# Second layer's rise of a fused mixer network: 18 of 22 pairs by seven block products for eight

## The chip, the cores and the metric

One core of one Trainium2 chip. The metric is the device time of one execution in microseconds, lower is better; a kernel's time is the median of its runs. TensorE is the matmul engine (PE in the profile), VectorE is DVE, ScalarE is ACT, GpSimd is POOL, and SyncE (SP) issues the weight transfers.

## What is computed

A first block (four mixers on 512 tokens of width 1024) and a second block of two layers; layer 0 of it also carries 256 context tokens, layer 1 works on the 512 tokens alone. Each layer of the second block ends with this part, and the change is in layer 1's:

```
h = rms_norm(x) * (1 + m4) + m3                 # 512 x 1024
z = h @ w_up                                    # 1024 x 5632, the "rise"
z = conv over tokens, width 3, per channel, + b
g, v = split(z)                                 # 2816 channels each
x = x + m5 * ((silu(g) * v) @ w_down)           # the "fall"
```

Everything is float32. Channels are taken in tiles of 128: a "pair" is a gate tile and its value tile, 22 pairs make the 2816 hidden channels.

## The kernel before

Channels lie on the partitions, tokens on the free axis. TensorE multiplies in a rounded form of float32, so every product is made of three (`three_products`, lines 225 to 227): each operand is split into a high part (a cast) and a low part (the rest), and high x high, high x low and low x high are added in PSUM. Weights come in *units* of 128 x 1024 (512 KB): all input channels for one tile of output channels, as eight weight tiles of 128 x 128. `stream_weights` (line 278) issues the units on SyncE's queue into a ring of four slots, each when a slot has been used. ScalarE casts a unit from the ring (`split_high`, line 479) into one of two buffers, VectorE subtracts (`split_low`, line 487) and thereby frees the slot.

`feed_forward` (lines 2684 on) is used for both layers. The rise has 44 units, gate and value tile of a pair in turn. A unit of layer 1 is 24 matmuls of 512 columns into one PSUM bank. VectorE then makes the convolution from the bank (centre tap with bias, line 2796, and two side taps, line 2801), ScalarE the Silu of a gate tile (line 2766), VectorE the product into `hidden` (line 2813). The first two units are opened in parts (lines 590 and 593), since h's high parts are ready before its low parts. VectorE makes h_low in line 430; before that stands the norm (line 425). The fall follows with 22 units, two of hidden's tiles at a time, in two halves of four banks; its moving operands are split two units ahead, and the results are added to x (line 2983) and stored. The order of work on each engine is the order in which the code emits it, all engines are in order, and every hand-over is a semaphore counted.

Elsewhere the change touches: the start of `build`, where POOL, once x and the constants are in, issues three tables (line 3138); behind that `recur_and_project`, where POOL issues `lora` (line 1399) and, after the normed x is split, `lru_w` (line 1401), for both of which TensorE waits at line 1455, after the third unit of steady work, ahead of the matmuls of lines 1459 and 1460; POOL's mask products in the scan stage (line 1629), two groups of chunks; and POOL's part of layer 0's feed-forward (silu_rows, lines 2718 to 2730, fetched again in line 2867).

## Time and profile before

| what | value |
|---|---|
| median of three runs | 2077.84 us |
| lowest, highest | 2071.98, 2082.45 us |
| the profiled execution, span | 2070.4 us |
| TensorE, VectorE, ScalarE, GpSimd busy | 97%, 63%, 36%, 4% of the span |
| granted TensorE clock, mean | 0.989 |
| weight loads (SyncE's queue) | 317 of 512 KB |

The page gives no time of the profiled execution beside its span, from its first to its last instruction; it is 1.6 us under the lowest timed run. Matmuls are pipelined: a matmul of 512 columns is drawn 0.39 us long and the next starts 0.23 us after it, so starts are what is to be compared. The granted clock is a share of the full 2.4 GHz. A row of a view that groups by line shows count, busy time, mean ns of one, and then the engine's idle time ahead of the group with what ended it.

### The profile page before, as it was taken

What the parts mean: (1) busy time and instruction counts of PE and PEld (TensorE: products, weight loads), DVE (VectorE), ACT (ScalarE), POOL (GpSimd) and SP (SyncE); (2) the same over time, 40 slices, a digit from 0 to 9 for tenths busy, and PEclk for the clock granted to TensorE, in tenths of its full rate; (3) what the DMA queues carried; (4) which work ended last, traced back from release to release, by engine and by line L of the source; (5) the groups of instructions that cost most, each with busy time, mean ns of one, the idle gap of its engine ahead of it and who ended that gap; (6) DMA issues with size and microseconds to landing.
All of it is one profiled execution on the core that took longest, in us unless ns stands there. A gap on an engine that the chain in (4) does not pass through costs nothing.

```text
span 2070.4 us, 29947 instructions
## 1 busy us (share of the span) xinstructions
PE 2014.7 (97%) x11473; PEld 1635.4 (79%) x11473; DVE 1296.3 (63%) x2091; ACT 738.3 (36%) x1188; POOL 84.1 (4%) x156
## 2 busy tenths in 40 slices
PE   7999999999999899999999999999999999999999
PEld 6677776577788678788888888887787778888887
DVE  6764424656548684688877664556477757766644
ACT  6621113744356452411111122334365432222332
POOL 0001000000130000000000000000310000000000
PEclk9989998999999999999999999999999999999999
DMA  5112125522362301233334233333543022223232
GB/s 200 64 62 103 62 103 183 197 88 84 134 176 65 127 1 51 92 109 129 128 128 134 83 112 122 102 112 102 156 129 118 4 89 83 100 91 101 94 100 81
DMA packets 57669, 217.43 MB, mean 105 GB/s; under 512 B 7440, under 2 KB 7440, under 8 KB 56416
## 3 DMA queue, kind: packets, MB, share of 16 engines
q1 hardware_dynamic: 46752, 168.32, 24.5%
q0 software_dynamic: 9296, 44.86, 6.7%
q10 hardware_dynamic: 1520, 2.85, 0.4%
q8 instruction: 72, 1.18, 0.2%
q14 instruction: 29, 0.24, 0.0%
HBM read 200.78 MB, written 15.20 MB: 104 GB/s over the span
## 4 chain that ended last, share of the span: by engine, by line
PE 88%; DVE 7%; ACT 3%; issue 2%; ACTq 0%; DVEq 0%
PE psum L225 23%; PE psum L226 22%; PE psum L227 22%; PE psum L816 3%; PE psum L590 2%; PE psum L777 2%; PE psum L804 2%; PE psum L1517 1%; PE psum L2013 1%; PE psum L2141 1%; PE psum L233 1%; PE psum L593 1%; PE psum L2547 1%; DVE neg_max L848 1%; PE psum L1543 1%
## 5 line engine op out<-in xcount | busy, mean ns | idle before, releaser
L225 PE MATMUL psum<-h_high,unit_high 128*128 128x512 f32 (+1 forms) x1704 | 620.6, 364 | 5.1 <-DVE unit_low L1390 4.5
L226 PE MATMUL psum<-h_low,unit_high 128*128 128x512 f32 (+1 forms) x1704 | 611.1, 359 | 0.0
L227 PE MATMUL psum<-h_high,unit_low 128*128 128x512 f32 (+1 forms) x1704 | 609.7, 358 | 0.0
L479 ACT CAST unit_high<-ring 128x1024 fp32r<-128x1024 f32 x196 | 205.4, 1048 | 563.6 <-PE psum L227 557.2
L225 PEld LDWEIGHTS psum<-h_high,unit_high 128*128 128x128 f32 x1704 | 322.1, 189 | 62.3 <-issue 5.3
L487 DVE TENSOR_TENSOR unit_low<-ring,unit_high 128x1024 fp32r<-128x1024 f32 x196 | 239.4, 1221 | 195.3 <-ACT unit_high L479 195.3
L226 PEld LDWEIGHTS psum<-h_low,unit_high 128*128 128x128 f32 x1704 | 322.4, 189 | 48.6 <-issue 2.8
L227 PEld LDWEIGHTS psum<-h_high,unit_low 128*128 128x128 f32 x1704 | 322.3, 189 | 48.6
L2801 DVE SCALAR_TENSOR_TENSOR conv_out<-psum,parameters,conv_out 128x511 f32<-128x511 f32 (+1 forms) x264 | 166.3, 658 | 21.3 <-DVE conv_out L2796 5.7
L2796 DVE TENSOR_SCALAR conv_out<-psum,parameters 128x512 f32<-128x512 f32 (+1 forms) x132 | 91.2, 719 | 113.4 <-PE psum L227 110.9
L889 ACT ACTIVATE probs<-psum,neg_max 128x768 f32<-128x768 f32 (+4 forms) x136 | 98.6, 728 | 129.4 <-DVE neg_max L848 117.2
L848 DVE TENSOR_REDUCE neg_max<-psum 128x1 f32<-128x768 f32 (+4 forms) x136 | 97.3, 740 | 27.6 <-PE psum L777 26.5
L816 PE MATMUL psum<-v,turned 128*128 128x64 f32 x784 | 99.2, 270 | 0.5 <-DVE v L866 0.5
L816 PEld LDWEIGHTS psum<-v,turned 128*128 128x128 f32 x784 | 96.0, 193 | 3.7 <-issue 1.8
L227 PE MATMUL psum<-y_high,unit_low 128*128 128x512 f32 (+1 forms) x256 | 93.6, 366 | 0.0
L225 PE MATMUL psum<-y_high,unit_high 128*128 128x512 f32 (+1 forms) x256 | 93.6, 366 | 0.0
L226 PE MATMUL psum<-hidden_part_low,unit_high 128*128 128x512 f32 (+1 forms) x264 | 93.5, 354 | 0.0
L226 PE MATMUL psum<-y_low,unit_high 128*128 128x512 f32 (+1 forms) x256 | 93.4, 365 | 0.0
L227 PE MATMUL psum<-hidden_part_high,unit_low 128*128 128x512 f32 (+1 forms) x264 | 93.1, 353 | 0.0
L225 PE MATMUL psum<-hidden_part_high,unit_high 128*128 128x512 f32 (+1 forms) x264 | 92.9, 352 | 0.0
L225 PE MATMUL psum<-unit_high,h_high 128*128 128x512 f32 x176 | 77.0, 438 | 0.0
L2766 ACT ACTIVATE conv_out<-conv_out 128x768 f32<-128x768 f32 (+1 forms) x44 | 32.6, 741 | 104.3 <-DVE conv_out L2801 104.3
(445 smaller groups left out, 2816.7 us busy)
## 6 DMA issues: line engine op xcount, KB each, us to landing
ring<-in_w_units SPq DMA_DIRECT2D x317, 512.0 KB, 3.5
stacked_heads<-head_parts POOLq DMA_DIRECT2D x48, 192.0 KB, 5.0
x_apart<-xT POOLq DMA_DIRECT2D x1, 3072.0 KB, 10.2
bias<-in_na_bias POOLq DMA_DIRECT2D x2, 1536.0 KB, 9.0
xT<-x_apart POOLq DMA_DIRECT2D x1, 3072.0 KB, 10.3
head_parts<-head_parts_high POOLq DMA_DIRECT2D x6, 384.0 KB, 6.2
head_parts<-p POOLq DMA_DIRECT2D x6, 384.0 KB, 6.0
xT<-in_x ACTq DMA_DIRECT2D x4, 512.0 KB, 6.0
```

Source lines behind the costliest of these rows:

```text
L225: pe.matmul(out, lh, rh, start=first, stop=False, skip_group_check=True)
L226: pe.matmul(out, lh, rl, start=False, stop=False, skip_group_check=True)
L227: return pe.matmul(out, ll, rh, start=False, stop=last, skip_group_check=True)
L479: act.copy(K.w_high[:, (K.unit + j) % 2], source).then_inc(K.high_split.sem, 1)
L487: dve.tensor_tensor(K.w_low[:, q % 2], K.ring[:, e % RING], K.w_high[:, q % 2].bitcast(F32), ALU.subtract).then_inc(K.unit_used.sem, 1)
L590: mm = pe.matmul(K.ps[bank][:, 0:b - a], high, moving[part][:, k, a:b], start=(k == 0 and part == 0), stop=(k == KD - 1 and part == 1), sk ...
L777: mm = pe.matmul(score_tile(t, c, c0, c0 + w), lhs, rhs, start=(g == 0), stop=(g == len(group) - 1), skip_group_check=len(group) > 1)
L816: mm = pe.matmul(K.ps[6][:, 0:HD], turned[:, t % 2, b * P:b * P + P], items[t]["v"](tile), start=(b == 0), stop=(b == len(tiles) - 1))
L848: max_ready.up(dve.reduce_max(neg_max[:, t, c:c + 1], score_tile(t, c, 0, kw), AX, negate=True))
L889: exped.up(act.activation(probs[:, t % depth, c, 0:kw], score_tile(t, c, 0, kw), ACT.Exp, bias=neg_max[:, t, c:c + 1], accum_out=row_sum[: ...
L2796: ins = dve.tensor_scalar(t(j, c0, c0 + w), bank[:, 0:w], column(wc + 44), column(bc), ALU.mult, ALU.add)
L2801: ins = dve.scalar_tensor_tensor(part, bank[:, src:src + w - 1], column(wc + 88 * (tap - 1)), part, ALU.mult, ALU.add)
```

## The change

18 of layer 1's 22 pairs leave the units. Their weights are cut in 2 x 2 blocks (input half by kind, gate or value), h in 2 x 2 blocks (input half by token half, 256 tokens), and a block product is made by Strassen's method in the form of Winograd: seven products instead of eight, with four sums of weight blocks (s1 = a21 + a22, s3 = a21 + a11, s2 = s1 + a11, s4 = s2 + a12; the signs are carried by h's sums and by the results) and four sums of h's blocks (T1 to T4). A *turn* takes two pairs, 7 *steps*; a step is 24 matmuls of 256 columns, 12 for each pair. The first four pairs stay whole units.

The weight sums are made in HBM by transfers of POOL's queue: copies of a21 to s1 and s3 right behind the three tables at the start, accumulations of a22 and a11 ahead of the second group of mask products, and in layer 0's feed-forward, behind silu_rows, copy and accumulation for s2 and then for s4, each waiting for the one before. T1 to T4 and their low parts are made by VectorE, their high parts by ScalarE, between norm and rise. Weight units of the rise have four buffers instead of two. Centre taps move from VectorE to ScalarE; results of the seven products go over three pairs of banks and are joined in a buffer `block_out`, from which the taps read. The fall is a function of its own, the same for both layers but for what its opening waits for. The rise of layer 1 is written out in full, with no hardware loop.

```diff
+SINGLE = 4
+TURN_PAIRS = 2
+B_TURNS = (KF - SINGLE) // TURN_PAIRS
+B_STEPS = 7
+LEFT, HALF_K = ("a11", "a12", "s2", "s1", "s3", "s4", "a22"), KD // 2 * P
+STORED, SUMMED = ("a11", "a12", "a21", "a22"), ("s1", "s2", "s3", "s4")
...
+            if n_units <= u < n_units + B_UNITS:
+                turn, step = divmod(u - n_units, B_STEPS)
+                if u == n_units:
+                    sp.wait_ge(K.signals["sums_made"].sem, 16 * len(SUMMED))
+                source = block_rows(K, LEFT[step])[TURN_PAIRS * turn:TURN_PAIRS * turn + TURN_PAIRS]
+                source, slot = source.rearrange("e p c -> p e c"), slot.rearrange("p (e c) -> p e c", e=TURN_PAIRS)
...
+def sum_blocks(K, pool, to, name, add):
+
+    rows = lambda x: block_rows(K, x).rearrange("t (q f) c -> (t q) (f c)", f=4)
+    if add:
+        return pool.dma_start(rows(to), rows(name), accum_op=ALU.add, max_dma_last_dim=8192)
+    return pool.dma_start(rows(to), rows(name))
...
     def _(pool):
         for g in range(NT // 2):
+            if g:
+                pool.wait_ge(sig["sums_copied"].sem, sig["sums_copied"].n)
+                for to, added_block in (("s1", "a22"), ("s3", "a11")):
+                    sig["sums_made"].up(sum_blocks(K, pool, to, added_block, True), 16)
             for lev in range(1, STEPS):
...
                 rows_out.up(pool.dma_start(K.silu_rows, rows_up[:, 0:2]), 16)
+                copied, made = K.signals["sums_copied"], K.signals["sums_made"]
+                for to, copy, addend in (("s2", "s1", "a11"), ("s4", "s2", "a12")):
+                    pool.wait_ge(made.sem, made.n)
+                    copied.up(sum_blocks(K, pool, to, copy, False), 16)
+                    pool.wait_ge(copied.sem, copied.n)
+                    made.up(sum_blocks(K, pool, to, addend, True), 16)
...
                 K.loaded_rest.up(pool.dma_start(dst, src), 16)
+            for to in ("s1", "s3"):
+                K.signals["sums_copied"].up(sum_blocks(K, pool, to, "a21", False), 16)
```

The new rise, engine by engine (`feed_forward_in_blocks`). TensorE, a turn:

```diff
+                    pe.wait_ge(K.unit_used.sem, first + n + 1)
...
+                    elif step == 1 and turn:
+                        pe.wait_ge(c11_out.sem, c11_out.base + turn)
...
+                    elif step == 2:
+                        pe.wait_ge(first_out.sem, first_out.base + turn + 1)
+                    elif step == 3 and turn:
+                        pe.wait_ge(c12_out.sem, c12_out.base + turn)
...
+                    elif step == 4:
+                        pe.wait_ge(second_out.sem, second_out.base + turn + 1)
+                    elif step == 5:
+                        pe.wait_ge(fifth_out.sem, fifth_out.base + turn + 1)
+                    elif step == 6:
+                        pe.wait_ge(c22_out.sem, c22_out.base + turn + 1)
...
+                    bank = (Y(turn), X, Y(turn), Z, Y(turn), Z, Y(turn))[step]
...
+                            mm = three_products(pe, K.ps[bank + e][:, 0:HS], (upper[:, c], lower[:, c]), x,
+                                                step in (0, 1, 3) and k == 0, k == KD // 2 - 1)
+                    product.up(mm)
```

VectorE's opening (T1 to T4 and the whole units), and its turn:

```diff
+            low(dve, 2)
+            side_tap.up(dve.tensor_tensor(total(T1), block(0, 0), block(0, 1), ALU.subtract))
+            link(dve, side_tap, dve.tensor_tensor(step_up, shift(4, 4), shift(0, 4), ALU.subtract))
+            for k in range(4):
+                side_tap.up(dve.scalar_tensor_tensor(total(T3)[:, k, :], block(1, 1)[:, k, :], step_up[:, k:k + 1],
+                                                     block(0, 1)[:, k, :], ALU.add, ALU.subtract))
+            low(dve, 3)
...
+            total_low(T3, 1.0, 2)
+            for n in range(2 * SINGLE):
+                taps(n // 2, n % 2, K.ps[n][:, :])
                 if n >= 2:
+                    low(dve, n + 2)
+                if n % 2:
+                    put_hidden(n // 2)
...
+                    if step == 5:
+                        unit_finished(dve, n - 1)
+                        dve.wait_ge(fifth_out.sem, fifth_out.base + turn + 1)
...
+                        c22_out.up(dve.scalar_tensor_tensor(C_out[:, 1, :, HS:S], both(Y(turn)), -1.0, fifth_part,
+                                                            ALU.mult, ALU.subtract))
+                    if step == 6:
+                        unit_finished(dve, n - 1)
+                        dve.wait_ge(second_out.sem, second_out.base + turn + 1)
+                        c12_out.up(dve.tensor_tensor(C_out[:, 0, :, HS:S], second_part, both(Z), ALU.add))
+                    if n + 2 < LAST:
+                        low(dve, n + 2)
...
+                    if step < 2 and turn:
+                        gate_tile(before, step)
+                    if step == 2 and turn:
+                        value_tile(before, 0)
+                    if step == 3:
+                        unit_finished(dve, n - 2)
+                        dve.wait_ge(first_out.sem, first_out.base + turn + 1)
...
+                        c11_out.up(dve.tensor_tensor(C_out[:, 0, :, 0:HS], first_part, both(X), ALU.add))
+                        if turn:
+                            value_tile(before, 1, (0,))
+                    if step == 4 and turn:
+                        value_tile(before, 1, (1,))
+                        put_hidden(SINGLE + TURN_PAIRS * before)
+                    if step == 5 and turn:
+                        put_hidden(SINGLE + TURN_PAIRS * before + 1)
```

ScalarE's opening and turn:

```diff
+            high(act, 2, None)
+            high(act, 3, None)
+            total_up(T1, 1.0, 1)
+            total_up(T3, 1.0, 6)
+            for n in range(2 * SINGLE):
+                unit_finished(act, n)
...
+                centre(n // 2, n % 2, K.ps[n][:, :])
+                if n < 2 * SINGLE - 1:
+                    high(act, n + 4, None)
+                if n % 2:
+                    soft(n // 2)
+                if n == 0:
+                    total_up(T2, -1.0, 10)
+                    total_up(T4, -1.0, 14)
...
+                    if step == 0 and turn:
+                        value_out(turn - 1)
+                    if step == 1:
+                        unit_finished(act, n - 1)
+                        act.wait_ge(c11_out.sem, c11_out.base + turn)
+                        first_out.up(act.copy(first_part, both(Y(turn))))
...
+                    if n + 3 < LAST:
+                        high(act, n + 3, n - 1)
...
+                    if step < 2 and turn:
+                        value_in(turn - 1, step)
+                    if step == 2 and turn:
+                        for e in range(TURN_PAIRS):
+                            soft(SINGLE + TURN_PAIRS * (turn - 1) + e)
+                    if step == 6:
+                        gate_in(turn)
```

## Rows read from the trace of the kernel before

**Rows 1.** The page, busy time and share of the span by engine
```profile
PE 2014.7 (97%) x11473; PEld 1635.4 (79%) x11473; DVE 1296.3 (63%) x2091; ACT 738.3 (36%) x1188; POOL 84.1 (4%) x156
```

**Rows 2.** The chain that ended last, from 1700 us on, shares by line
```profile
by line: PE psum L226 31.9%; PE psum L225 31.8%; PE psum L227 31.2%; PE psum L590 1.9%; PE psum L593 1.0%; DVE unit_low L487 0.3%; ACT unit_high L479 0.3%; DVE hidden L425 0.2%; DVE xT L2983 0.2%; ACT h_high L413 0.2%; ACT hidden L410 0.2%;
```

**Rows 3.** Windows: length; busy PE, PEld, DVE, ACT, POOL; PEclk, DMA share, GB/s
```profile
14.40:24.00 9.60, 7.40 (x35) 5.55 (x34) 5.64 (x9) 6.00 (x11) 0.49 (x2) 1.00 1.03 401
24.00:55.00 31.00, 29.90 (x130) 24.05 (x129) 25.02 (x34) 15.75 (x28) 0.57 (x1) 1.00 0.30 96
328.00:336.00 8.00, 8.00 (x28) 2.50 (x28) 3.37 (x9) 3.39 (x9) 0.00 (x0) 0.52 1.03 382
140.00:148.00 8.00, 8.00 (x28) 6.81 (x27) 4.28 (x15) 0.00 (x0) 0.63 (x1) 0.50 0.00 0
1715.00:1945.00 230.00, 229.79 (x1003) 188.41 (x1004) 161.27 (x193) 59.32 (x66) 0.00 (x0) 1.00 0.29 96
```

**Rows 4.** Timeline, TensorE: first matmul of the rise's third unit; first of the fall
```profile
1715.21 0.50 PE L225 MATMUL psum<-h_high,unit_high 128*128 128x512 f32 x1 [0.62 <-DVE unit_low L487]
...
1946.16 0.39 PE L225 MATMUL psum<-hidden_part_high,unit_high 128*128 128x512 f32 x1
```

**Rows 5.** Timeline, TensorE, layer 0: 24 matmuls of 256 columns, first and successor
```profile
1150.63 0.28 PE L225 MATMUL psum<-h_high,unit_high 128*128 128x256 f32 x1
...
1153.36 0.39 PE L225 MATMUL psum<-h_high,unit_high 128*128 128x512 f32 x1
```

**Rows 6.** Groups by line, VectorE, from 1700 us on
```profile
L487 DVE TENSOR_TENSOR unit_low<-ring,unit_high 128x1024 fp32r<-128x1024 f32 x64 | 78.1, 1220 | 58.5 <-ACT unit_high L479 58.5
L2801 DVE SCALAR_TENSOR_TENSOR conv_out<-psum,parameters,conv_out 128x511 f32<-128x511 f32 x88 | 66.0, 750 | 11.1 <-DVE conv_out L2796 1.4 <-DVE conv_out L2801 1.4
```

**Rows 7.** Timeline, VectorE, in the unrolled end of the rise
```profile
1936.22 1.53 DVE L2801 SCALAR_TENSOR_TENSOR conv_out<-psum,parameters,conv_out 128x511 f32<-128x511 f32 x2
1937.79 0.69 DVE L2813 TENSOR_TENSOR hidden<-conv_out 128x512 f32<-128x512 f32 x1
1938.40 1.22 DVE L487 TENSOR_TENSOR unit_low<-ring,unit_high 128x1024 fp32r<-128x1024 f32 x1
```

**Rows 8.** Groups by line, ScalarE: casts, gates, and copies out of PSUM
```profile
L479 ACT CAST unit_high<-ring 128x1024 fp32r<-128x1024 f32 x64 | 67.3, 1052 | 206.5 <-PE psum L227 200.2 <-PE psum L590 6.4
L2766 ACT ACTIVATE conv_out<-conv_out 128x512 f32<-128x512 f32 x22 | 14.0, 635 | 38.4 <-DVE conv_out L2801 38.4
L1942 ACT ACTIVATE p<-psum 128x512 f32<-128x512 f32 x8 | 4.8, 597 | 73.8 <-PE psum L227 73.8
```

**Rows 9.** DMA issues: count, KB each, median us from issue to landing
```profile
ring<-in_w_units SPq DMA_DIRECT2D x317, 512.0 KB, 3.5
xT<-in_x POOLq DMA_DIRECT2D x1, 2048.0 KB, 8.9
...
xT<-in_ctx POOLq DMA_DIRECT2D x1, 1024.0 KB, 11.9
```

**Rows 10.** Timeline at the opening of layer 1's rise
```profile
1705.62 5.39 DVE L430 SCALAR_TENSOR_TENSOR h_low<-hidden,mods,h_high 128x512 fp32r<-128x512 f32 x8
1713.91 1.28 ACT L2766 ACT_TABLE_LOAD   x1
```

**Rows 11.** Timeline, POOL's loads of lora and lru_w, and TensorE behind line 1455's wait
```profile
14.35 0.54 POOL L1399 DMA_DIRECT2D sums<-in_lora  x1
37.70 0.57 POOL L1401 DMA_DIRECT2D xT<-in_lru_w  x1 [22.81 <-DVE h_low L367]
...
55.25 1.02 PE L1459 MATMUL psum<-xT 128*128 128x512 f32 x2
```

**Rows 12.** Timeline, POOL: ahead of the second group of masks, and layer 0's feed-forward
```profile
235.33 0.64 POOL L1629 TENSOR_TENSOR p<-xT,constants_first 128x256 f32<-128x256 f32 x1 [55.42 <-DVE xT L1749]
...
871.79 0.54 POOL L2730 DMA_DIRECT2D silu_rows<-hidden  x1 [18.55 <-ACT hidden L2725]
1219.52 0.53 POOL L2867 DMA_DIRECT2D silu_rows<-silu_rows  x1 [347.19 <-PE psum L227]
```

More of the change, by code:

```diff
@@ L2681, in entries, with feed_forward @@
     return [n + sum(m < n for m in behind) for n in range(count + RING + 1)]
-def feed_forward(K, layer, with_ctx, sums, out, c_rows=None):
-    W = S + C if with_ctx else S
+def feed_forward(K, layer, sums, c_rows):
+    with_ctx, W = True, S + C
     conv, gate_done = K.signals["conv"], K.signals["silu"]
@@ L2911, in _ @@
-            for a in (0, half):
-                unit(0, a)
-                with pe.Fori(0, 2) as i:
-                    for j in range(RING):
-                        unit(i, a + 1 + j, 1)
-                unit(0, a + 9)
-                unit(0, a + 10)
+            open_latents(K, pe, first, h, waits[0]).then_inc(K.unit_done.sem, 1)
+            opening_part(K, pe, first + 1, 1, h, 0, 1).then_inc(K.unit_done.sem, 1)
+            for n in range(2, 2 * SINGLE):
+                pe.wait_ge(K.unit_used.sem, first + n + 1)
+                upper, lower = room(n)
+                for k in range(KD):
+                    c = slice(k * P, k * P + P)
+                    mm = three_products(pe, K.ps[n][:, :], (upper[:, c], lower[:, c]), tuple(m[:, k, :] for m in h),
+                                        k == 0, k == KD - 1)
+                mm.then_inc(K.unit_done.sem, 1)
@@ new lines, in soft, with gate_in @@
+            def soft(p):
+                act.wait_ge(gate_taps.sem, gate_taps.base + p + 1)
+                gate_done.up(act.activation(t[2 * (p % 2)], t[2 * (p % 2)], ACT.Silu))
+            def gate_in(turn):
+                for e in range(TURN_PAIRS):
+                    p = SINGLE + TURN_PAIRS * turn + e
+                    act.wait_ge(hid_put.sem, hid_put.base + p - 1)
+                    act.wait_ge(c12_out.sem, c12_out.base + turn + 1)
+                    centre(p, 0, C_out[:, 0, e, :])
@@ new lines, in taps, with gate_tile @@
+            def taps(p, kind, source, which=(0, 1)):
+                centred = (gate_centre, value_centre)[kind]
+                for last in which:
+                    if last:
+                        dve.wait_ge(side_tap.sem, side_tap.n)
+                    else:
+                        dve.wait_ge(centred.sem, centred.base + p + 1)
+                    tap(p, kind, last, source)
+            def gate_tile(turn, e):
+                taps(SINGLE + TURN_PAIRS * turn + e, 0, C_out[:, 0, e, :])
@@ new lines, in _ @@
+            last = B_TURNS - 1
+            for e in range(TURN_PAIRS):
+                gate_tile(last, e)
+            for e in range(TURN_PAIRS):
+                value_tile(last, e)
+                put_hidden(KF - TURN_PAIRS + e)
+        K.unit_used.n += LAST
+        K.high_split.n += LAST
+        K.unit_done.n += 2 * SINGLE
+        K.unit += LAST
+        ends = c11_out, c12_out
+        openings = [(ends[o // 2].sem, ends[o // 2].n) for o in range(4)]
+        all_put = (hid_put.sem, hid_put.n - TURN_PAIRS), (hid_put.sem, hid_put.n)
@@ L3051 @@
+        halfway = (c21_out.sem, c21_out.n)
+        start_phase(K)
+        fall(K, layer, False, hidden, mv, None, out, all_put, openings, halfway)
 SIGNALS = ("met", "act_step", "dve_step", "conv_step", "unit_used", "loaded_late", "unit_done", "high_split",
@@ L3487, in lay_out @@
         else:
-            units += [rising, falling]
+            units += [rising[:2 * SINGLE], falling]
+            blocks = rising[2 * SINGLE:].reshape(KF - SINGLE, 2, P, 2, HALF_K).transpose(1, 3, 0, 2, 4)
     w_units = np.concatenate(units)
```

519 lines of the change are left out of this document (367 added, 152 removed).

## The prediction

> **What bounds the kernel now.** I read four views, in this order. The page's busy times: TensorE is busy 97% of the span, VectorE 63% [rows 1]. The chain that ended last, for the last 371 us: it is TensorE's three products almost alone, 95% in lines 225 to 227 [rows 2]. The windows: from 1715 to 1945 us, the second layer's rise after its first two units, TensorE is busy 229.8 of 230 us at full clock, VectorE 161, ScalarE 59, and the DMA engines carry 96 GB/s [rows 3]. So there only fewer columns through TensorE can help. Last, what a column costs: 42 units run from 1715.21 to 1946.16 [rows 4], 5.499 us each, 229.1 ns per matmul of 512 columns. In layer 0, 24 successive matmuls of 256 columns take 1150.63 to 1153.36 [rows 5], 113.8 ns each, with a new weight tile for each. Half the columns cost half the time, also with weight loads twice as often.
>
> **The sum, part by part.**
>
> 1. Products. 36 of the 44 units go: 864 matmuls x 0.2291 = 198.0 us. They become 9 turns x 7 steps x 24 = 1512 matmuls of 256 columns x 0.1138 = 172.0 us. Gain 26.0 us, 1/8 less 1.1 us of fixed cost.
> The Trainium skill (TensorE: Matmul & The Clock Gate, Back-to-back issue gap) gives columns/2.4 + 2.5 ns per matmul, 215.8 and 109.2 ns here, by which the gain would be 186.5 - 165.1 = 21.4 us. The rows are 6% and 4% above that rule, and I go by them.
>
> 2. Do the other engines keep up? A step of TensorE is 2.73 us, a turn 19.1 us. VectorE in a turn has 7 weight lows of 1.22 us, 8 taps of 0.75 [rows 6], three evacuations (0.75 at most) and two products of 0.69 [rows 7]: 18.2 us. Starts in the unrolled end of the old rise lie closer than durations (0.61 for the 0.69 one, 1.57 for two taps that wait for each other [rows 7]), so it will be some 17.1 us, 2 us of slack. It was 3.9 of 5.5 us per unit. ScalarE: 7 casts x 1.05, 4 centres, 4 evacuations and 2 gates of 0.6 to 0.7 [rows 8], 13.7 us of 19.1. The handovers: a product's bank is copied out by ScalarE (0.6 us) or VectorE (0.75 us) during the one step of 2.73 us that TensorE works in other banks, at the head of their queues; four weight slots let VectorE's split be two steps ahead. Behind these waits stand splits for two or three steps later and taps for the last turn, with 3 us to spare. I cost the turns' waits at 0; if VectorE took 20 us, it would be 9 x 0.9 = 8 us. Weights: 512 KB per 2.73 us, 192 GB/s, landing in 3.5 us [rows 9]; the load of a slot starts some three steps (8 us) before its cast. Cost 0.
>
> 3. Opening of the rise: a loss. VectorE is done with h_low at 1711.0 [rows 10]. Then come two splits, T1 and two lows of sums (5 x 1.14) and twelve sums on 256 columns (estimate, half of 0.75: 0.4 each), 10.7 us, to 1721.7; four taps 3.0; the first product waits for the gate, whose table load (1.28 [rows 10]) now stands behind the casts of the sums, to 1726.1; centre and taps of unit 2, 1.5, and only then the split of unit 4: 1728.8. TensorE, which starts unit 2 some 0.6 us earlier than now (the wait at 1715.21 goes [rows 4]), wants unit 4 at 1714.6 + 2 x 5.5 = 1725.6. It waits 3.2 us. At the first turn, step 1's split stands behind unit 7's centre and taps (3.4 us after the unit, 2.7 there): 0.7. Sum +3.3; from 0 (if T1 to T4 fit beside) to +6.
> End of the rise: the fall's first unit wants banks and splits that are ready a step before; 0, at most 1.
>
> 4. The first copies, the large unknown. POOL issues lora at 14.35 us, behind three tables, and lru_w at 37.70; TensorE waits for both ahead of line 1459, and gets there at 55.25 without waiting [rows 11]. Between tables and lora the change puts two copies of 18 x 128 x 512 x 4 bytes = 4.72 MB, HBM to HBM, on the same queue. That queue is served in order as far as the trace shows: x and ctx, 2048 and 1024 KB issued together, land after 8.9 and 11.9 us [rows 9]. So both loads come after 9.44 MB. The engines' pace when full is 382 GB/s (share 1.03 [rows 3]). What they carry already from 14.4 to 55 us is 401 x 9.6 + 96 x 31 = 6.8 MB [rows 3], 18 us at that pace. No row has an HBM to HBM copy. If it runs like a load, 9.44 MB take 25 us: lora lands at 14.4 + 18 + 25 = 57, and TensorE waits 2 us. If a byte counts twice, once read and once written, 49 us: it lands at 82, a wait of 26 us. Both ends come from the same row, and nothing is nearer to one of them. I take the middle, 37 us: landing at 69, a wait of 14 us. Nothing hides it: the next units are queued behind the wait in order, and what VectorE and ScalarE do there feeds on TensorE's results. After 14 us of standing the granted clock will have fallen: it was 0.50 for the whole of 140 to 148 us, with TensorE busy again [rows 3]. Some 6 us at half, 3 us lost. Together +17, bounds +2 and +30.
> The Trainium skill (DMA: Bandwidth & Descriptors, Latency and other measured facts) has HBM to HBM copies at 207 to 214 GB/s per direction; by that 9.44 MB take 45 us and the wait is 22 us, 8 more than mine. The trace shows no such copy.
>
> 5. The other sums. The two accumulations are issued by POOL at about 180 us, where it stands idle until 235.33 [rows 12], so its masks aren't late; they are beside weight loads at 95 GB/s. Layer 0's two copies and two accumulations run from 872 us; POOL waits inside for each, and next has to issue at 1219.52 [rows 12], 347 us later. Ring loads there have about 11 us of slack over the 3.5 they take. An accumulation reads two streams and writes one, for 4.72 MB each 25 to 75 us, and fits in both places. Cost +1, bounds 0 and +8 (late modulation pairs in the scan stage).
>
> Sum: -26.0 + 3.3 + 17 + 1 = **-4.7 us**. The profiled execution has a span of 2070.4 us; the three timed runs are 2071.98 to 2082.45, median 2077.84, so the median is 7.4 above the span. Predicted span 2065.7, median 2073. About 0.5% (10 us) is what a measurement of this kernel can tell from no change.
>
> **Rivals.**
> A, the copies are quick. Under 32 us for both (295 GB/s up), the wait is under 9 us and the change is faster by over 0.5%. For it: loads reach 382 GB/s. Against: a copy uses the memory twice. Time: -26 + 3.3 + 2 + 1 = -20, 2058. Chance 0.33.
> B, the copies are slow, and it ends slower. The place is line 1455's wait, the price one us for each us of landing after 55; it decides from 84 us on, a pace below 180 GB/s. At 140 GB/s they take 67 us: wait 44, clock 4, the change +26, 2104. For it: the bytes are counted twice, and the first ten us are full already. Against: 192 GB/s is enough to avoid it. Chance 0.15.
> C, the turns don't run at TensorE's pace: VectorE's in-order queue or a copy-out delays each turn by a us or more. For it: VectorE at 90%. Against: no single wait is nearer than a us. +9: 2082. Chance 0.10.
> D, the products aren't fewer columns in effect, a weight load per 256 columns binding over a long stretch: against it the 24 in a row. Chance 0.02, 2099.
> The forecast itself, copies between 32 and 52 us and the turns at pace: chance 0.40, its own range 2065 to 2086.
>
> **The numbers.** Faster is A and a small part of the forecast, 0.38. Same is the rest of the forecast and most of C, 0.43. Slower is B, D and the rest of C, 0.19. Range: low, A with the opening at +1, 2056; high, the bytes counted twice with the opening at 6, contention 4: -26 + 6 + 30 + 4 = +14, 2092, and 2 more towards B: 2094.
>
> **What would show it.** Right: matmuls of 256 columns 0.114 us apart and steps at 2.73; a stop of TensorE at line 1455's wait put down to the DMA of lora or lru_w, and that DMA landing at 60 to 80 us; one wait of some 3 us for the split of unit 4; VectorE busy under 18 us per turn; nothing at 180 to 280 us. Wrong: no stop at 55 us (A), one of over 30 (B), waits inside every turn (C), TensorE waiting for POOL or ring loads beside the accumulations.

## The result, and the profile after

The changed kernel is slower. Its median is 2093.16 us beside 2081.31 for the kernel before, 20 executions each; the ratio is 1.0056, with a 95% interval of 1.0033 to 1.0080. Forecast were 2073 us and a ratio of 0.998. Two of the changed kernel's executions, at 2469 and 5330 us, were in a slower state; the ratio leaves them out. The two profiled executions stand further apart than the medians: spans of 2092.2 and 2070.4 us, 21.8 us. Why single executions scatter by several us is told at the end.

Where the 21.8 us are is read from POOL's timeline, because POOL's transfers mark the stages in both kernels.

```profile
37.70 0.59 POOL L1430 DMA_DIRECT2D xT<-in_lru_w  x1 [21.14 <-DVE h_low L396]
...
892.20 0.54 POOL L2763 DMA_DIRECT2D silu_rows<-hidden  x1 [18.54 <-ACT hidden L2758]
892.73 0.54 POOL L311 DMA_DIRECT2D block_sums<-block_sums  x1
913.36 1.11 POOL L310 DMA_DIRECT2D block_sums<-in_w_blocks  x1 [20.09 <-DMA block_sums<-block_sums]
944.22 0.53 POOL L311 DMA_DIRECT2D block_sums<-block_sums  x1 [29.76 <-DMA block_sums<-in_w_blocks]
963.02 1.06 POOL L310 DMA_DIRECT2D block_sums<-in_w_blocks  x1 [18.26 <-DMA block_sums<-block_sums]
1252.56 0.57 POOL L2906 DMA_DIRECT2D silu_rows<-silu_rows  x1 [288.48 <-PE psum L234]
```

Against [rows 11, 12], lru_w is issued at the same 37.70. Layer 0's rise begins at 892.2 where it began at 871.8 (+20.4) and ends at 1252.6 where it ended at 1219.5 (+33.0). The fall adds 4.6 more, and layer 1 begins 37.6 us late. The end comes 21.8 us late, so the second layer gives back 15.8. **The blocks do gain; what comes before them costs more than twice that, and the experiments put it down to the transfers that make their weight sums.** This table has every kernel of the study by the same marks, in us. The first column is the time of the first transfer of x into x_apart, the end of the first block; the others are lengths. The last runs from layer 1's load of dft to the end of the span. The two stretches left out take 177 and 143 us in all of them (178 in e11). Each row is one execution; e2, e3, e4, e6, e7, e10, e11 and e12 were run once only, so of these the stretches are read and not the total.

| kernel | first block ends | dft to layer 0's rise | layer 0's rise | fall, to x_apart | last stretch | span |
|---|---|---|---|---|---|---|
| before | 513.7 | 181.2 | 347.7 | 219.4 | 488.8 | 2070.4 |
| after | 534.2 | 181.2 | 360.4 | 224.0 | 473.0 | 2092.2 |
| e1, no sums | 512.7 | 188.8 | 347.7 | 219.4 | 475.6 | 2063.9 |
| e2, low buffers | 526.7 | 188.6 | 360.7 | 221.7 | 473.2 | 2090.8 |
| e3, small rows | 530.6 | 187.3 | 349.9 | 219.5 | 473.2 | 2080.1 |
| e4, late copies | 524.1 | 181.2 | 354.9 | 219.4 | 475.3 | 2074.6 |
| e5, small copies | 521.5 | 188.7 | 352.8 | 224.4 | 473.1 | 2080.0 |
| e6, extra aligned | 531.3 | 188.6 | 358.2 | 224.0 | 469.3 | 2091.1 |
| e7, all aligned | 526.2 | 187.2 | 363.7 | 224.5 | 479.5 | 2101.0 |
| e8, e5 + e7 | 519.4 | 185.6 | 357.2 | 225.0 | 481.1 | 2087.7 |
| e9, three edits | 509.3 | 185.5 | 347.7 | 219.8 | 468.5 | 2050.1 |
| e10, before + sums | 537.4 | 188.6 | 359.3 | 224.0 | 488.8 | 2117.6 |
| e11, gap of 32 | 512.2 | 181.1 | 358.9 | 225.8 | 480.1 | 2078.9 |
| e12, mirrored | 513.1 | 187.2 | 357.1 | 225.0 | 475.2 | 2077.1 |

**What TensorE waits for.** The chain that ended last, by line, was TensorE's products and little else; the page of after has a new member, a weight load into the ring.

```profile
PE psum L232 20%; PE psum L234 20%; PE psum L233 20%; DMA ring<-in_w_units 6%; PE psum L845 3%; PE psum L806 2%; PE psum L833 2%; PE psum L619 2%; PE psum L1546 1%; PE psum L2174 1%; PE psum L240 1%; PE psum L2046 1%; PE psum L2580 1%; PE psum L622 1%; DVE neg_max L877 1%
```

The waits from 24 to 70 us, columns: who waited, for what, us in total, times, longest:

```profile
ACT unit_high L1413 <- DMA ring<-in_w_units: 12.0, 2, 10.9
PE psum L232 <- DVE unit_low L1419: 9.5, 2, 8.4
```

and from 892 to 1010 us:

```profile
ACT unit_high L508 <- DMA ring<-in_w_units: 59.6, 8, 15.8
POOL block_sums L310 <- DMA block_sums<-block_sums: 38.4, 2, 20.1
POOL block_sums L311 <- DMA block_sums<-in_w_blocks: 29.8, 1, 29.8
...
PE psum L232 <- DVE unit_low L516: 5.3, 3, 3.8
```

ScalarE's cast waits for a weight load, VectorE's split for the cast, TensorE for the split. Line 1488, which stands behind the wait for lora and lru_w, starts at 65.3 in after and at 55.25 before [rows 11]; but lora landed at 54.1 and lru_w at 55.6, and no wait is put down to them. How long the ring's loads took in after from issue to landing (min/median/max, of those issued from 14 to 70 us; then from 185 to 270; then from 880 to 1050):

```profile
DMA to landing us min/median/max: 3.5/17.9/30.7
...
DMA to landing us min/median/max: 3.4/18.3/25.5
...
DMA to landing us min/median/max: 3.5/9.6/18.9
```

In the kernel before the first of these reads 3.3/3.5/5.0. Two windows show the second price of the stops, in the last but two column: the granted clock falls.

```profile
24.00:55.00 31.00, 21.50 (x88) 16.83 (x87) 17.82 (x26) 13.77 (x26) 0.59 (x1) 0.90 0.97 335
...
892.00:1010.00 118.00, 112.67 (x643) 98.49 (x642) 94.68 (x145) 20.15 (x21) 3.76 (x5) 0.97 0.93 272
```

From 24 to 55 us TensorE is busy 21.5 us instead of 29.9, at 0.90 instead of full clock, while the DMA engines carry 335 GB/s instead of 96 [rows 3]. Over the whole first block TensorE's waits add up to 36 us instead of 25, and the granted clock is at its lower level (1.2 GHz, 0.50) for 61 us instead of 41, which at half speed costs up to 10 us: the two together account for the 20.4.

Layer 0's rise can be added up in the same way. Its 12.7 us are 5.3 us of waits for splits (three of them), 3.4 us of clock (half speed from 963.8 to 970.7, behind the longest wait), and some 4 us because most of its matmuls of 256 columns start each 117.8 ns and not 113.3. The 4.6 us of the fall are of this last kind: TensorE waits for no load or split there, but a unit takes 8.43 us instead of 8.21. This higher interval is told at the end; it isn't shown to come from the transfers.

**The second layer's rise.** Between the first matmul of 256 columns (1789.66) and the fall's first (1967.11) TensorE waits once, for 0.7 us; the 1512 matmuls take the other 176.7 us, 116.9 ns each, and not 113.8 [rows 5]. The timeline shows why; these are the first matmuls of three successive pairs of steps, 48 matmuls apart:

```profile
1796.23 0.28 PE L232 MATMUL psum<-totals_high,more_units_high 128*128 128x256 f32 x1
...
1801.99 0.28 PE L232 MATMUL psum<-totals_high,unit_high 128*128 128x256 f32 x1
...
1807.42 0.28 PE L232 MATMUL psum<-totals_high,more_units_high 128*128 128x256 f32 x1
```

5.76 us (120.0 ns each) from the extra buffers, 5.43 (113.1) from the old two; over all nine turns the means are 120.0 and 113.5.

### The profile page after: what moved, and what is told of

It is laid out like the page before. It is cut to its first block, busy times and chain, and to the rows that moved or that the text cites. A ratio compares the mean times of both kernels' runs of the same rounds, so it can differ in the third digit from the quotient of the medians.

```text
span 2092.2 us, 30953 instructions
## 1 busy us (share of the span) xinstructions
PE 2015.8 (96%) x12121; PEld 1665.0 (80%) x12121; DVE 1316.2 (63%) x2119; ACT 816.9 (39%) x1299; POOL 90.6 (4%) x164
## 4 chain that ended last, share of the span: by engine, by line
PE 79%; DVE 9%; DMA 6%; ACT 4%; issue 2%; ACTq 0%; DVEq 0%; SPq 0%
PE psum L232 20%; PE psum L234 20%; PE psum L233 20%; DMA ring<-in_w_units 6%; PE psum L845 3%; PE psum L806 2%; PE psum L833 2%; PE psum L619 2%; PE psum L1546 1%; PE psum L2174 1%; PE psum L240 1%; PE psum L2046 1%; PE psum L2580 1%; PE psum L622 1%; DVE neg_max L877 1%
## 5 line engine op out<-in xcount | busy, mean ns | idle before, releaser
L232 PE MATMUL psum<-h_high,unit_high 128*128 128x512 f32 (+1 forms) x1416 | 501.4, 354 | 22.0 <-DVE unit_low L1419 12.9
L233 PE MATMUL psum<-h_low,unit_high 128*128 128x512 f32 (+1 forms) x1416 | 487.3, 344 | 0.0
L234 PE MATMUL psum<-h_high,unit_low 128*128 128x512 f32 (+1 forms) x1416 | 487.1, 344 | 0.0
L516 DVE TENSOR_TENSOR unit_low<-ring,unit_high 128x1024 fp32r<-128x1024 f32 x152 | 185.8, 1223 | 203.7 <-ACT unit_high L508 203.7
L232 PE MATMUL psum<-totals_high,unit_high 128*128 128x512 f32 (+1 forms) x312 | 106.9, 343 | 0.5 <-DVE totals_low L3019 0.5
L2840 DVE SCALAR_TENSOR_TENSOR conv_out<-psum,parameters,conv_out 128x511 f32<-128x511 f32 (+1 forms) x176 | 100.3, 612 | 10.2 <-DVE conv_out L2835 4.3
L234 PE MATMUL psum<-totals_high,unit_low 128*128 128x512 f32 (+1 forms) x312 | 106.6, 342 | 0.0
L233 PE MATMUL psum<-totals_low,unit_high 128*128 128x512 f32 (+1 forms) x312 | 105.9, 339 | 0.0
L2835 DVE TENSOR_SCALAR conv_out<-psum,parameters 128x512 f32<-128x512 f32 x88 | 55.6, 673 | 56.6 <-PE psum L234 56.0
L234 PE MATMUL psum<-unit_high,h_low 128*128 128x512 f32 x176 | 69.5, 395 | 0.0
```

What stands on the lines that cost most here:

```text
L232: pe.matmul(out, lh, rh, start=first, stop=False, skip_group_check=True)
L233: pe.matmul(out, lh, rl, start=False, stop=False, skip_group_check=True)
L234: return pe.matmul(out, ll, rh, start=False, stop=last, skip_group_check=True)
L516: dve.tensor_tensor(K.w_low[:, q % 2], K.ring[:, e % RING], K.w_high[:, q % 2].bitcast(F32), ALU.subtract).then_inc(K.unit_used.sem, 1)
L2835: ins = dve.tensor_scalar(t(j, c0, c0 + w), bank[:, 0:w], column(wc + 44), column(bc), ALU.mult, ALU.add)
L2840: ins = dve.scalar_tensor_tensor(part, bank[:, src:src + w - 1], column(wc + 88 * (tap - 1)), part, ALU.mult, ALU.add)
```

## The experiments

**1. Without the sums.** The transfers of `sum_blocks` and the waits for them go, and `block_rows` takes stored blocks for s1 to s4:

```diff
-    return K.w_blocks[STORED.index(name)] if name in STORED else K.block_sums[SUMMED.index(name)]
+    return K.w_blocks[STORED.index(name)] if name in STORED else K.w_blocks[SUMMED.index(name)]
```

> The changed kernel without the twelve transfers that make s1 to s4; the steps that took the sums load stored blocks of the same size instead, so the rise computes other numbers in the same time. Theory (the transfers starve the four-slot weight ring while they are in flight): all of the 37.6 us that the changed kernel is late at the end of layer 0 goes: +10 at line 1488, +10 by 262, +17 in layer 0's feed-forward. The gain of the block products, 15.8 us, stays: a span near 2055, 0.990 to 0.994 of the kernel before. Rival (the lateness has another cause, such as the longer program or the issue on POOL's queue in the loads' shadow): most of the 37 us stays, 2075 to 2092. Rival (in the second layer's rise itself the loads from the sums are slow): the rise too gets faster than 177.4 us.

The lateness is gone: the first block ends at 512.7, layer 0's rise takes 347.7 us and the fall 219.4, as before. The ratio is 0.9909, interval 0.9875 to 0.9942, some 19 us faster than before; with +12 for the changed kernel, the transfers (eight of them, not twelve) cost about 31 us at the median, less than the 37.6 of the one execution. The profiled span is 9 us above what was expected, 7.6 of it in the stretch from dft to the rise, where the clock was lower (see the end). The rise is no faster (177.5 us), so loads from the sums aren't slow. They need not be: in after they land in 3.6 us at the median.

**2. The sums alone, in the kernel before** (nine weight units stand in for each block, same bytes, rows and places, and nothing reads the sums):

```diff
+            for to in ("s1", "s3"):
+                K.signals["sums_copied"].up(sum_blocks(K, pool, to, "a21", False), 16)
```

and likewise the accumulations and layer 0's four transfers (not shown here).

> The kernel before with nothing but the eight transfers (copies and accumulations of 4608 KB, same rows, same places in POOL's order, of weight units that nothing reads). Theory (the transfers alone cost what the changed kernel loses before its rise): later by 6 to 12 us at line 1459's place, 16 to 22 by 513 us and 29 to 38 by the end of layer 0, span 2099 to 2108. Rival (something else of the changed program has a part): less than 24 us.

The first block ends 23.7 us late, layer 0's rise takes 11.6 more and the fall 4.6 more: 39.9 us, and the last stretch is the 488.8 of before. The first two figures are above the 16 to 22 and 29 to 38 us expected, and the span has 7.4 us more from dft to the rise. The loss is there without the changed program, so no other part of that program is needed to explain it.

**3. Rows of 2 KB for the sums.**

```diff
-    rows = lambda x: block_rows(K, x).rearrange("t (q f) c -> (t q) (f c)", f=4)
+    rows = lambda x: block_rows(K, x).rearrange("t (q f) c -> (t q) (f c)", f=1)
-        return pool.dma_start(rows(to), rows(name), accum_op=ALU.add, max_dma_last_dim=8192)
+        return pool.dma_start(rows(to), rows(name), accum_op=ALU.add, max_dma_last_dim=2048)
```

> The changed kernel with the sums' transfers in rows of 2 KB instead of 8 KB, the same bytes. Theory a (the ring's loads, in 4 KB rows, share the DMA engines row by row with 8 KB rows of the sums): with 2 KB rows the loads get a larger share, a ring load beside a copy lands in well under the 18 us it takes now, and layer 0's end comes at +15 to +25 instead of +37.6; the copies themselves take longer. Theory b (the loads are slow because memory traffic is at its limit of some 250 to 290 GB/s whatever the rows): ring loads stay near 18 us and the lateness near 37, or grows as the small rows make the transfers longer.

Half of it fell out as theory a has it, in a telling way. POOL's queue, packets and MB, of after and then of this kernel:

```profile
q0 software_dynamic: 12112, 82.60, 13.6%
```
```profile
q0 software_dynamic: 19024, 82.60, 14.3%
```

Before had 9296 packets. The rest is 9728 = 4 accumulations x 2304 rows + 512: the four copies stay at 128 packets each, 36 KB apiece, whatever rows they are written in. And where accumulations run, the ring's loads are quick now (185 to 270 us: median 7.2, at most 10.6, instead of 18.3 and 25.5), where copies run they aren't (14 to 70 us: at most 31.7). Layer 0's rise loses 2.2 us instead of 12.7; the start, with its copies, is as late as ever (POOL issues the accumulations at 191.95, in after at 189.93). By the end of the first block it is 16.9 us late instead of 20.4. The bytes are the same. Nor is it that the traffic is thinner: from 190 to 245 us the engines are full in both, and carry nearly the same (after, then this kernel):

```profile
190.00:245.00 55.00, 51.78 (x421) 39.35 (x422) 12.16 (x28) 6.08 (x10) 2.17 (x2) 0.86 1.00 235
```
```profile
190.00:245.00 55.00, 54.33 (x503) 41.92 (x503) 14.63 (x34) 8.15 (x14) 5.22 (x4) 0.97 1.01 227
```

So it is the packet's size and not the traffic.

**4. Rows of 2 KB for the copies too.**

```diff
-    return pool.dma_start(rows(to), rows(name))
+    return pool.dma_start(rows(to), rows(name), max_dma_last_dim=2048)
```

> The changed kernel with the accumulations in rows of 2 KB and the copies too held to 2 KB (with 2 KB rows asked of the accumulations alone, the page counts 9728 packets for the sums' eight transfers: 9216 for the accumulations and 512 for the four copies, 36 KB each). Theory (a ring load's 4 KB packets stand behind the POOL queue's big packets on each DMA engine, so what matters is the size of those packets): the packets of q0 rise to about 27700, ring loads beside the copies land in under 11 us instead of up to 31, the 10 to 12 us at the start and the 5 us of the copies in layer 0 nearly go; the span comes to 2065 to 2075 and the time to 0.990 to 0.998 of the kernel before. Rival (the copies load the memory itself, whatever the packets): the start stays 10 us late, span near 2080.

POOL's queue has 23248 packets: the copies are in (23248 - 9296 - 9216) / 4 = 1184 packets of 4 KB, fewer than expected, but small. Ring loads now take, in the same three stretches:

```profile
DMA to landing us min/median/max: 3.5/7.6/10.7
...
DMA to landing us min/median/max: 3.6/7.1/10.7
...
DMA to landing us min/median/max: 3.4/6.8/10.9
```

The ratio is 0.9956, interval 0.9931 to 0.9981: the small rows alone make the changed kernel faster than before. The two copies, 38 us in big packets, now take 46 in all, and with small rows comes the wait that the prediction had expected in the changed kernel itself:

```profile
PE psum L1488 <- DMA xT<-in_lru_w: 5.5, 1, 5.5
```

Layer 0's rise has not one wait for a load; its 5.1 us more are of another kind, told at the end.

**5. The copies behind lora and lru_w.**

```diff
         K.loaded_late.up(pool.dma_start(lru_w, K.lru_w_dram.rearrange("p (a b) -> p a b", a=4)), 16)
+        for to in ("s1", "s3"):
+            K.signals["sums_copied"].up(sum_blocks(K, pool, to, "a21", False), 16)
```

> The changed kernel with the two first copies (s1 and s3 from a21) issued behind lora and lru_w on POOL's queue instead of ahead of them. The prediction's reason (TensorE waits at line 1488 for lora or lru_w behind the copies): line 1488 comes at 55 as in the kernel before and the 10 us are gone for good. Theory now (the copies starve the weight ring, whoever stands behind them): line 1488 comes near 55 too or a little late, but the copies now run from 38 to 76, the ring loads of that stretch land late, and by 190 us the kernel is again 5 to 12 us late; the span moves by no more than 5 us.

Missed on the size: the span moved by 17.6 us, and not by 5 at most. The accumulations are issued at 181.1, where before POOL stands idle from 179.9 [rows 12] and after issues at 189.9: the copies now cost about 1 us, though a load still takes up to 30.7 us to land beside them. Between 38 and 72 us the ring's slack covers that, between 15 and 53 it doesn't. The first block still ends 10.4 us late, 9 of it from the accumulations on.

**6. Where the extra buffers stand.** First they were put below hidden instead of behind the totals; only addresses differ:

```diff
+        wx = arena_pair(K, ctx, "more_units", [P, 2, KD * P])
         hid = arena(K, ctx, "hidden", [P, KF, S])
         h = arena_pair(K, ctx, "h", [P, KD, S])
         totals = arena_pair(K, ctx, "totals", [P, 4, KD // 2, HS])
-        wx = arena_pair(K, ctx, "more_units", [P, 2, KD * P])
```

> The changed kernel with the two extra weight buffers put at the start of the second layer's region, below hidden, in place of the region behind the totals; no instruction differs but in addresses. In the changed kernel a matmul of 256 columns starts every 120.0 ns when its weights lie in the extra buffers and every 113.3 ns when they lie in the old two, turn after turn. Theory (the place of the buffer in SBUF, near the moving operand, costs the 6.7 ns): all steps run at 113.3, the rise from the first 256-column matmul to the fall goes from 177.4 to near 172.5, the span falls by 5. Rival (it is the unit's number, ring slot or order of work, not the address): 120.0 stays for half of the steps.

The 120.0 ns stayed, in the same steps. Both places begin at 64 modulo 128 bytes of a partition's row, the old two buffers at 0; h and the totals at 64. So a gap of 64 bytes:

```diff
+        arena(K, ctx, "gap", [P, 16])
         wx = arena_pair(K, ctx, "more_units", [P, 2, KD * P])
```

> The changed kernel with a gap of 64 bytes ahead of the extra weight buffers. With these buffers at another place, below hidden, the 120.0 ns stayed; both places begin at 64 modulo 128 bytes in each partition's row, the old two at 0. Theory (a weight tile that begins in the middle of a 128-byte line is read slower): with the gap all steps start a matmul each 113.3 ns and the rise takes 5 us less. Rival (order of the units): 120.0 stays for every other pair of steps.

Now every pair of steps takes 113.3 ns a matmul and the rise 172.6 us instead of 177.4. The six kernels with the extra buffers at 64 and the operands at 64 have 177.4 to 177.6, the two with the gap before these buffers alone 172.6. Groups by line inside the rise, of after and of this kernel (count, busy us, mean ns of one as it is drawn):

```profile
L232 PE MATMUL psum<-totals_high,more_units_high 128*128 128x256 f32 x149 | 42.2, 283 | 0.0
L232 PE MATMUL psum<-totals_high,unit_high 128*128 128x256 f32 x136 | 37.5, 276 | 0.0
```
```profile
L232 PE MATMUL psum<-totals_high,more_units_high 128*128 128x256 f32 x144 | 39.7, 276 | 0.0
L232 PE MATMUL psum<-totals_high,unit_high 128*128 128x256 f32 x135 | 37.3, 276 | 0.0
```

"A weight tile must begin at 0" was still the wrong rule. The gap ahead of everything overlaid, so that the moving operands begin at 0 as well:

```diff
+        arena(K, ctx, "gap", [P, 16])
         first = ctx.enter_context(ExitStack())
```

> The changed kernel with a gap of 64 bytes ahead of everything that is overlaid, so that the moving operands too (h, the totals, hidden's parts) begin at 0 modulo 128. Same theory as for the gap before the extra buffers alone, for the second layer's rise: 5 us less. For the rest of the kernel it is a question: 256-column matmuls of layer 0's rise start each 113.4 or 117.8 ns from one stall to the next, in the same buffers; if that is an effect of the operands' place they all run at 113.4 or less and the stretch of layer 0's rise and fall (567.1 us in the kernel before) is never longer than there; if it is not, both levels stay.

All steps now take 118.6 to 119.9 ns, layer 0's matmuls of 256 columns 118.6 to 119.2, and the span is 2101.0, the longest of the changed kernels. The same gap and the small rows of experiment 4:

> Both edits together: every overlaid buffer moved by 64 bytes, and 2 KB rows for all of the sums' transfers. If both theories hold the parts add up: a span of 2060 to 2070, the time 0.988 to 0.995 of the kernel before, 3 to 6 us under the one with small rows alone. If only that of the packets holds, it equals the one with small rows alone.

Ratio 1.0038, interval 1.0011 to 1.0064: the gap takes back 17 of the some 21 us that the small rows give (medians of 2089.8 and 2073.2 us), far from the parts adding up as expected. Then the three edits of experiment 7, but with 32 bytes ahead of everything and 32 more before the extra buffers:

> The kernel with the three edits, but with everything overlaid moved by 32 bytes (moving operands at 96 modulo 128, the extra buffers brought to 0 by another 32). Known by now: weights at 0 and moving operand at 64, a matmul of 256 columns starts each 113.3 ns in the written-out rise and either 113.4 or 117.8 ns in layer 0's loop; both at the same place modulo 128, 119 to 120 ns. Theory (only the half of the 128-byte line counts, and 96 is the same half as 64): all as with the three edits. Rival (the finer place counts): another interval than 113.3 in the second layer's rise, or one level alone in layer 0's.

The rival held: 118 to 120 ns in both rises, at a span of 2078.9. And the mirror image, 64 bytes ahead of everything and 64 more before the extra buffers:

> The kernel with the three edits, with everything overlaid moved by 64 bytes: moving operands at 0 modulo 128, the old two weight buffers at 0, the extra two at 64. Known: 113.3 ns with weights at 0 and moving operand at 64; 119 to 120 with both at 0, both at 64, or weights at 0 and moving at 96. Theory (what matters is that weight tile and moving operand stand half a 128-byte line apart): in the second layer's rise the steps from the extra buffers start a matmul each 113.3 ns (or 117.8), the steps from the old two each 119 to 120; layer 0's loops at 118 to 120. Rival (only weights at 0 with the moving operand at 64 is fast): every step at 118 to 120.

As the theory says, within a ns. Inside the rise, in groups as above:

```profile
L232 PE MATMUL psum<-totals_high,more_units_high 128*128 128x256 f32 x123 | 34.0, 277 | 0.0
L232 PE MATMUL psum<-totals_high,unit_high 128*128 128x256 f32 x120 | 33.7, 281 | 0.0
```

From the extra buffers (64, moving at 0) 113.7 ns, from the old two (0, moving at 0) 118.5.

**7. The three edits together**: small rows for all transfers, copies behind lru_w, the gap before the extra buffers alone.

> The changed kernel with 2 KB rows for all of the sums' transfers, the first two copies issued behind lora and lru_w, and the gap of 64 bytes before the extra weight buffers. Theory: the start loses nothing beside the kernel before (the 5.5 us for which TensorE waited for lru_w behind small-row copies go, ring loads land within 11 us and the ring covers that), layer 0's rise only what its 256-column matmuls lose where they run at 117.8 ns (0 to 5 us), the second layer's rise takes 172.6 us from the first 256-column matmul to the fall. Span 2048 to 2062, time 0.984 to 0.991 of the kernel before. Rival (the copies, 38 to 80 us in, still hold up the ring in a stretch with two thirds of the loads of the whole start): 5 to 8 us at the start stay, span 2056 to 2068.

It beats the kernel before: the ratio is 0.9899, interval 0.9873 to 0.9926, median 2058.7 us beside 2079.96. Its profiled execution is the quickest of its six, in part by luck: in the first block the clock is at its lower level for 24 us, in before for 41. On its own timeline layer 0's rise, with the same four transfers beside it, is as long as before [rows 12]:

```profile
871.71 0.54 POOL L2765 DMA_DIRECT2D silu_rows<-hidden  x1 [18.55 <-ACT hidden L2760]
...
1219.45 0.57 POOL L2908 DMA_DIRECT2D silu_rows<-silu_rows  x1 [256.15 <-PE psum L234]
```

From 24 to 55 us TensorE is busy as in [rows 3], with 2.3 times the traffic:

```profile
24.00:55.00 31.00, 29.89 (x130) 24.03 (x129) 25.00 (x34) 15.75 (x28) 2.80 (x3) 1.00 0.67 225
```

## Why the prediction was wrong

The gain was forecast rightly, but for one term; the losses were not. The steps that failed are the fourth and, above all, the fifth: what the sums' transfers do to the ring's loads.

1. **Products: right, one term mis-sized.** Sized at 0.1138 us each, 172.0 in all; they took 176.7, 4.7 more. The row was of weights and moving operand 64 bytes apart modulo 128; half of the new steps have them at the same place. With the gap it is 172.6, its wait included. (The gain of 26.0 is an eighth of 198 and 1.2 us more, not less, since 113.8 ns is under half of 229.1.) The rule of the Trainium skill (TensorE: Matmul & The Clock Gate, Back-to-back issue gap) gives 109.2 ns, and that is below every interval seen here.
2. **Turns: right.** No step but the first turn's waits. VectorE is busy 134.5 of 155 us inside e9's rise (1760 to 1915 us), 16.6 us a turn of 19.2 (17.1 expected). The ring's loads land there in 4.0 us at the median.
3. **Opening: right, 1.2 us short.** +3.3 expected, with two waits for splits of 3.2 and 0.7. From layer 1's load of dft to where the ninth unit begins in before it is 166.6 us, to the first matmul of 256 columns in after 170.4; with the wait behind it that is 4.5 us. The two waits of after are 3.1 and 0.7:

```profile
PE psum L232 <- DVE unit_low L3166: 3.8, 2, 3.1
```

4. **First copies: the size came near, the mechanism was wrong.** Expected was a stop of 14 us at the wait for lora and lru_w, +17 with the clock; measured +10 there, and through another wait. The pace of the copies was right: 9.44 MB in 38.7 us, 37 expected, and this is 244 GB/s. The Trainium skill (DMA: Bandwidth & Descriptors, Latency and other measured facts) has 207 to 214 GB/s per direction for copies of another layout, by which it would have been 45 us; the trace is quicker. Two steps failed. The 18 us of other traffic were put ahead of the copies, but they ran beside them, so lora came at 54 and not 69. And that traffic was the ring's: what it shared with the copies it lost, up to 30.7 us for a load that takes 3.5, and TensorE stopped for weights before it came to lora.
5. **The other sums: this step decides it.** Cost +1, bounds 0 and +8; measured +10.4 by 534 us, 12.7 in layer 0's rise and, in this execution, 4.6 in the fall, 27.7 together. Some 8.5 of these are the higher interval, which may not be the transfers' doing; the 19 left are still far outside the bounds. "Ring loads there have about 11 us of slack over the 3.5 they take" is sound only if loads go on taking 3.5 to 14 us beside the transfers. Issued beside the four transfers, from 892 to 994 us, they took 13.2 at the median and up to 18.9; beside the first two accumulations 18.3 and up to 25.5. A bandwidth sum (95 GB/s of loads, up to 382 possible) said that both fit; it doesn't say who is served first. And a stop of TensorE costs again in clock: from 920 to 980 us the mean is 0.94.

Sum: from layer 1 on -26.0 + 4.7 + 3.3 = -18.0, where -15.8 was measured. Of the other 2 us, 1.2 are in the opening, where the clock is at half from 1766.0 to 1769.4, behind the wait of 3.1 us, and 0.8 in the fall (125.1 us to the end instead of 124.2). e1 and e4 have 2.5 more in the last stretch, with the same rise: there the clock is at half for 6.8 us soon after the load of dft. Before layer 1 it is +10.0 + 10.4 + 12.7 + 4.6 = 37.7. None of the rivals had the loss. A wanted both copies in under 32 us, and they took 38 and, in small packets, 46; B put the price at lora. That 2093 us lies just inside the range, up to 2094, is luck: the range reached so far for slow copies and a wait at lora, neither of which came. "TensorE waiting for ring loads beside the accumulations" stood among the signs of being wrong, without a price. It should have been a rival.

## What to carry to other kernels

Beside a stream of loads that must land in time, a big transfer on another queue is to be costed by what it does to one load's landing, not by GB/s; cut its rows to the size of the loads' own or smaller (2 KB here), look at the page's packet count to see whether it was done, since the plain copies between HBM tensors went in 36 KB packets until they were limited, and issue it where the ring has slack. Before a matmul of few columns with a new weight tile each is costed from a row, see that the operands of that row and those of the new kernel lie at the same places modulo 128 bytes. And a change that is slower as built can still be faster once its side costs are found: here 1.0056 became 0.9899 with the same products.

## What the runs showed of the hardware

**A load waits by the size of the other queue's packets.** A 512 KB load lands in 3.5 us at the median with no such transfer beside it, in up to 32 beside 36 KB packets of another queue, up to 26 beside 8 KB ones, and in at most 13 beside those of 2 to 4 KB (12.9 in e12, 10.9 in e5). The Trainium skill (DMA: Bandwidth & Descriptors, Queues, rings and completion order) says that each engine goes round its queues and takes a whole packet from one before it turns to the next. The runs fit that, and these are the prices; but the page means by a packet a run of several descriptors, and whether that is what the profile counts isn't shown. The Trainium skill (Perfetto Trace Analysis, DMA Optimizations) advises to batch 2 KB transfers into 4 or 8 KB for throughput. The trace agrees on the throughput (an accumulation takes 38 us in small rows and 30 in large ones), but here the large rows cost more than they gave, because TensorE waits for the ring's loads and not for the sums.

**Matmuls of 256 columns and the places of the operands.** One starts each 113.3 ns (64 bytes apart modulo 128: weights at 0 and moving at 64, or 113.7 with 64 and 0), and each 118 to 120 ns in the other pairings tried (0 and 0, 64 and 64, 0 and 96). Matmuls of 512 columns go another way: in layer 1's whole units those from the extra buffers start each 227 ns at 64 and 64, and each 233 with the gap, so the gap gives 4.9 us in the steps and takes back some 0.6 ahead of them. The reason isn't known.

**Two levels for the same code.** Even at 0 and 64 there is a second level, 117.8 ns, in layer 0's loops. In layer 0's rise of after, 24 matmuls and their successor; [rows 5] has them in 2.73 us:

```profile
1099.28 0.28 PE L232 MATMUL psum<-h_high,unit_high 128*128 128x256 f32 x1
...
1102.10 0.40 PE L232 MATMUL psum<-h_high,unit_high 128*128 128x512 f32 x1
```

Here it is 2.82. At 941.09 the interval was 113; TensorE waited at 944.89, and at 950.51 it was 117.8. Most changes stand at a stop of TensorE, if only of 0.2 us, but not all: at 973.6 it was 117.8 and at 981.9 it was 113.3, with no stop between. A unit of the rise takes 8.33 us instead of 8.21, and in the fall 8.43 instead of 8.21. That is 4 to 5 us in the rise (352.8 instead of 347.7 in e5) and 4.6 in the fall. What sets the level isn't settled. The rise ran at the low one in before, e1 and e9, and at the high one in e5, where no wait for a load stands, and nearly all of e10; in after it ended high, in e3 and e4 it fell from high to low.

**The clock scatters too.** From dft to layer 0's rise it takes 181 us in four of the profiled executions and 185 to 189 in the others, with and without the sums. The mean granted clock there is 0.99 or 1.00 in the four and 0.94 to 0.96 in the others; in the first 29 us it is 0.76 in e5 and 1.00 in the kernel before, at the same traffic of 208 GB/s. What starts such an episode isn't settled. The kernel before ran from 2068 to 2094 us in its first 20 executions. In the 23 that stand beside e5 time and mean clock go together, from 2069 us at 0.991 to 2094 at 0.981 (correlation -0.74), so the clock is a large part of that scatter; how much the two levels add can't be told from one profile of that kernel. This is why a difference of 10 us can't be read from one execution of each.
